# Feed forwards: the second half of the scaled row goes to a PSUM bank, and GpSimd splits two weight sums behind the last crossed part

## The reference

```
def swiglu(h, w_in, w_out):
    g, u = jnp.split(h @ w_in, 2, axis=-1)
    return (jax.nn.silu(g) * u) @ w_out
...
        h = h + g2 * swiglu(modulate(h, norm2_g[l], sh2, sc2), ffn_w_in[l], ffn_w_out[l])
        if need_ctx:
            hc = hc + cg2 * swiglu(modulate(hc, norm2_g[l], csh2, csc2), ffn_w_in[l], ffn_w_out[l])
```

## Time and profile before

| | |
|---|---|
| median of 3 runs | 4000.85 us (4000.85 to 4006.97) |
| the profiled execution's own time | 4003.02 us |
| its span | 4000.9 us |
| TensorE busy | 3700.5 us (92%) |
| VectorE busy | 2337.9 us (58%) |
| GpSimd busy | 1802.7 us (45%) |
| ScalarE busy | 1505.0 us (38%) |

### The profile page before, as it was taken

How to read it: one execution, slowest core, us unless ns; L and a number is a source line. 1 busy time by engine, 2 the same in 40 slices (tenths; PEclk the granted TensorE clock), 3 DMA queues, 4 the chain that set the end, 5 groups by cost and what they waited for, 6 DMA issues and landing times. The chain is left out here.

```text
span 4000.9 us, 82113 instructions
## 1 busy us (share of the span) xinstructions
PE 3700.5 (92%) x33646; PEld 3242.0 (81%) x33646; DVE 2337.9 (58%) x4324; ACT 1505.0 (38%) x2826; POOL 1802.7 (45%) x1226
## 2 busy tenths in 40 slices
PE   6998899999899899989799999979999999988997
PEld 5877799999677788868698888769999878668996
DVE  3345566666553766685557775276666640637665
ACT  3235333333365443332234443243333241644443
POOL 2201455554344777632233432155555332737884
PEclk8999999999999999989879999889999989989998
DMA  4223233332201444432201100223333211012331
GB/s 177 69 98 106 90 101 112 119 108 95 70 5 48 152 154 154 137 112 109 76 20 31 29 21 25 80 85 106 106 116 114 72 63 64 23 54 74 101 101 63
DMA packets 159555, 343.99 MB, mean 86 GB/s; under 512 B 33487, under 2 KB 89295, under 8 KB 158799
## 3 DMA queue, kind: packets, MB, share of 16 engines
q1 hardware_dynamic: 139311, 266.37, 20.2%
q10 hardware_dynamic: 19872, 72.36, 5.3%
HBM read 323.88 MB, written 16.93 MB: 85 GB/s over the span
## 5 line engine op out<-in xcount | busy, mean ns | idle before, releaser
L1450 POOL TENSOR_TENSOR feed_low<-feed_sums,feed_high 128x512 fp32r<-128x512 f32 x320 | 502.0, 1587 | 476.0 <-ACT feed_high L1444 468.0
L1450 POOL TENSOR_TENSOR feed_low<-ring,feed_high 128x512 fp32r<-128x512 f32 x448 | 596.2, 1347 | 193.6 <-ACT feed_high L1444 96.7
L1444 ACT ACTIVATE feed_high<-ring 128x512 fp32r<-128x512 f32 x448 | 278.5, 626 | 433.2 <-PE ps L1692 243.2
L1676 PE MATMUL ps<-hn_high,feed_high 128*128 128x384 f32 (+1 forms) x1280 | 401.9, 314 | 0.8 <-ACT feed_gate L1764 0.8
L1677 PE MATMUL ps<-hn_low,feed_high 128*128 128x384 f32 (+1 forms) x1280 | 395.4, 309 | 0.0
L1678 PE MATMUL ps<-hn_high,feed_low 128*128 128x384 f32 (+1 forms) x1280 | 395.3, 309 | 0.0
L1690 PE MATMUL ps<-feed_hid,feed_high 128*128 128x384 f32 (+1 forms) x1056 | 378.8, 359 | 13.6 <-DVE h L1874 6.1
L1691 PE MATMUL ps<-feed_hid,feed_high 128*128 128x384 f32 (+1 forms) x1056 | 375.9, 356 | 0.0
L1692 PE MATMUL ps<-feed_hid,feed_low 128*128 128x384 f32 (+1 forms) x1056 | 375.5, 356 | 0.0
L1444 ACT ACTIVATE feed_high<-feed_sums 128x512 fp32r<-128x512 f32 x320 | 189.3, 626 | 488.5 <-DVE feed_sums L1469 275.0
L1676 PE MATMUL ps<-cross_high,feed_high 128*128 128x384 f32 (+1 forms) x960 | 300.3, 313 | 22.7 <-issue 21.7
(11 more groups left out here) (639 smaller groups left out, 9489.1 us busy)
## 6 DMA issues: line engine op xcount, KB each, us to landing
feed_side_ring<-in_ada ACTq DMA_DIRECT2D x138, 512.0 KB, 4.3
ring<-in_ffn_g SPq DMA_DIRECT2D x88, 512.0 KB, 4.9
ring<-in_ffn_u SPq DMA_DIRECT2D x88, 512.0 KB, 3.7
ring<-in_ffn_d SPq DMA_DIRECT2D x88, 512.0 KB, 3.8
diff_side_ring<-in_ada SPq DMA_DIRECT2D x32, 512.0 KB, 4.2
ring<-in_od_in SPq DMA_DIRECT2D x24, 512.0 KB, 4.0
ring<-in_ev_in SPq DMA_DIRECT2D x23, 512.0 KB, 5.2
ring<-in_even_in SPq DMA_DIRECT2D x20, 512.0 KB, 4.1
```

The lines of the kernel that those rows point to most:

```text
L1444: act.activation(self.high[:, e % self.SLOTS, :], self.source(name, n), ACT.Copy).then_inc(self.high_ready, 1)
L1450: pool.tensor_tensor(self.low[:, slot, :], self.source(name, n), self.high[:, slot, :].bitcast(F32), ALU.subtract).then_inc(self.low_ready, 1)
L1676: pe.matmul(dst, high, vh, start=c == 0, stop=False)
```

## The change

It has three edits, all in the feed forward:
- `cross` scales the first half of the row into the SBUF scratch as before, and the second half into PSUM bank 6. All that reads the second half reads it there. The scaling is cut at half the tokens, so it has one instruction more in each part.
- The scratch handed to it is only half as wide.
- GpSimd's loop leaves out operand 11 after part 3. Operands 11 and 12 are split after the low part of part 4.

```
--- before.py
+++ after.py
     def cross(self, dve, c):
 
-        h, upper, lower = self.half, self.scratch, self.sq[:, c, :]
+        h, first, second, lower = self.half, self.scratch, self.k.ps[:, 6, 0:self.half], self.sq[:, c, :]
...
-        for a, b, s in spans(self.tokens):
-            dve.scalar_tensor_tensor(out=upper[:, a:b], in0=self.k.h[:, c, a:b], scalar=self.gains[:, c, s:s + 1],
-                                     in1=self.root[:, a:b], op0=ALU.mult, op1=ALU.mult)
+        for a, b, s in [(0, h, 0)] + self.second_half():
+            dve.scalar_tensor_tensor(out=second[:, a - h:b - h] if a else first, in0=self.k.h[:, c, a:b],
+                                     scalar=self.gains[:, c, s:s + 1], in1=self.root[:, a:b], op0=ALU.mult, op1=ALU.mult)
         dve.drain()
         for a, b, s in self.second_half():
             if s:
-                dve.scalar_tensor_tensor(out=t1[:, a - h:b - h], in0=upper[:, a:b], scalar=self.context_shifts[:, c:c + 1],
-                                         in1=upper[:, a - h:b - h], op0=ALU.add, op1=ALU.subtract)
+                dve.scalar_tensor_tensor(out=t1[:, a - h:b - h], in0=second[:, a - h:b - h], scalar=self.context_shifts[:, c:c + 1],
+                                         in1=first[:, a - h:b - h], op0=ALU.add, op1=ALU.subtract)
             else:
-                dve.tensor_tensor(t1[:, a - h:b - h], upper[:, a:b], upper[:, a - h:b - h], ALU.subtract)
+                dve.tensor_tensor(t1[:, a - h:b - h], second[:, a - h:b - h], first[:, a - h:b - h], ALU.subtract)
         for a, b, s in self.second_half():
             step, op = (self.shifts[:, c, s:s + 1], ALU.subtract) if shifted else (self.step_shifts[:, c, s:s + 1], ALU.add)
-            dve.scalar_tensor_tensor(out=t3[:, a - h:b - h], in0=lower[:, a:b], scalar=step, in1=upper[:, a:b], op0=op, op1=ALU.subtract)
+            dve.scalar_tensor_tensor(out=t3[:, a - h:b - h], in0=lower[:, a:b], scalar=step, in1=second[:, a - h:b - h], op0=op, op1=ALU.subtract)
...
-            norm = stream(st, vectors=vectors, fourth=fourth, scratch=upper[:, :])
+            norm = stream(st, vectors=vectors, fourth=fourth, scratch=upper[:, 0:H])
...
                 norm.low_cross(pool, c)
                 if c == 0:
                     operands.write_low(pool, 8)
-                operands.write_low(pool, 9 + c)
+                if c < 2:
+                    operands.write_low(pool, 9 + c)
+            operands.write_low(pool, 11)
+            operands.write_low(pool, 12)
             norm.low_fourth(pool)
```

## The result

The changed kernel takes 3971.1 us (median of 4 runs, 3967.0 to 3975.6), the kernel before 4001.9 beside it (4 runs, 4000.9 to 4007.0). The ratio is 0.9914, 95% interval 0.9887 to 0.9942: 0.86% faster, where 0.55% was predicted. A second series of the changed kernel gave 3970.6 and 0.9924 (0.9911 to 0.9937). The direction was right, and most of the gain is in the place that I had named; it is 34 us by the first ratio and 30 by the second (the medians differ by 30.8 and 29.0), where I had 22.2.

A forecast was written before the change was run, and what follows sets the result against it. TensorE, busy mostly, stops 21.7 us in the feed forwards for VectorE's crossed parts, held by GpSimd's SBUF lock. Chain 17.5 plus clock 4.9 minus swap 0.2 gives 22.2 us: 4000.85 to 3978.6, range 3968 to 3990 (own range 3973 to 3985).

The forecast's parts named there:

- 19.2 us free: VectorE's L1350, L1347 and L1353 over four crossed stretches: their cost without waiting behind GpSimd, against 58.5 us measured before.
- Rival E: VectorE's scaled second half: writing it to PSUM is slow and makes the kernel slower, 4010 us at 1.3 us; chance 0.04.
- the chain gains, 17.5 us: VectorE's crossed parts ahead of TensorE's first crossed product: they end 5.3, 3.0, 5.9 and 3.3 us earlier in four stages.
- the 39.3 us of waiting: Time L1350, L1347 and L1353 stand still behind GpSimd in four crossed stretches; all of it was to go from them.
- My walk: First stage's four crossed parts, turn by turn, with `t2` and the fourth sum still waiting for GpSimd: ends 5.3 us earlier.
- The clock: TensorE's granted clock stays up behind the first and third stages' shortened stops, giving 4.9 us; the fourth stays slow.
- The GpSimd swap: Moving operand 11's split behind low part 4 delays later splits by 1.3 us; cost 0.2 us, bounds 0 and 5.2.
- The sum: Whole kernel: 17.5 + 4.9 - 0.2 = 22.2 us gained, from the median 4000.85 to 3978.6 us.
- C: Crossed stretches: hardly any waiting comes back, stops shrink to TensorE's own pace, 33.6 us gained, 3967 us; chance 0.12.
- B: Crossed parts: waits move on more than walked or the PSUM write is dear; chain gains 9, about 3988 us; chance 0.22.
- D: TensorE's stops are set by low part 4 and the plain product, not crossed parts: no change, 4000 us; chance 0.07.
- The PSUM source: `t1` and `t3` reading PSUM: taken as costing nothing extra; the skill's 65 ns each would add 3.1 us, giving 3981.7.

The follow-up runs named there:

- cut_in_sbuf: Changed kernel with the scaled row's second half kept in SBUF instead of PSUM, same cut and GpSimd order: 3988.2 us, ratio 0.9981 to the kernel before.
- swap_only: Kernel before with only GpSimd's new order (operands 11 and 12 split after low part 4), row uncut in SBUF: 4010.5 us, ratio 1.0014.
- one_locked_swap_long: Changed kernel with, at 512 tokens, one instruction per part with two SBUF inputs and GpSimd's old order: 3970.5 us, ratio 0.9923 to the kernel before.
- after_third: Changed kernel, unedited, traced once more to see whether its stages repeat: the execution took 3976.0 us.
- psum_only: Changed kernel with GpSimd's order as in the kernel before (operand 11 split between low parts 3 and 4): 3974.2 us, ratio 0.9950 to the kernel before.
- swap_long_only: Changed kernel with GpSimd's new order only at 768 tokens, the old order at 512: 3970.3 us, ratio 0.9932 to the kernel before.
- psum_long_only: Changed kernel with the second half in PSUM only at 768 tokens, in SBUF at 512: 3975.1 us, ratio 0.9936 to the kernel before.
- one_locked: Changed kernel rewritten at 512 tokens so one instruction behind the scaling, not two, has both inputs in SBUF: 3969.9 us, ratio 0.9919 to the kernel before.

## Why the prediction was right and wrong

**The mechanism: right.** Which instructions stop standing still and by how much (19.2 us free), and that `ps<-h` costs no more than a write to SBUF (0.48 us for 256 columns): as written. The added scaling instruction makes a part 0.13 us longer, where I had 0.18. Rival E is out. `cut_in_sbuf` shows that the PSUM input itself does it, 17 us of the feeds.

**The step that failed: the chain gains, 17.5 us.** From before to after the time from the start of the crossed stretch to the first crossed product shrank by 6.3, 2.9, 6.9 and 5.0 us, 21.1 in all, where I had 5.3, 3.0, 5.9 and 3.3. That is 54% of the 39.3 us of waiting, where I had written less than half. VectorE's four parts alone shrank by 6.4, 4.2, 6.9 and 5.0, 22.5 in all: in the second stage the parts gained 4.2, but TensorE no longer waited for them and moved by 2.9, so that it meets my 3.0 is luck. My walk had the turns of the first stage right and their sizes a little too dear. It has 6.1, 6.65, 5.25 and 5.2 us for the four parts; they took 5.92, 6.08, 5.09 and 5.09. Part 2 makes half of that: `t2` asked 0.15 us earlier than walked, and `t2` and the fourth sum then took 1.78 and 1.48 us, their own 0.74 and 0.62 included, less than I had for two whole splits. Summed up, I let 21.8 of the 39.3 us be lost again, 2.9 of them to the added instructions, and 18.2 were: 13.7 as waits of `t2` and the fourth sum, 2.1 for the added instructions, 1.3 in the second stage, the rest in gaps. So the term that was too large is the waiting that comes back: some 19 us walked, 13.7 measured.

**The clock: right in size, then given back elsewhere.** Behind the first and third stop it stays 1.00, 2.4 us each by the matmuls of these two traces, as predicted. For the third stage that was the price of one execution: in the other two traces of the kernel before the clock there was 1.00 and 0.68 already. And a stop of 2.04 us that comes 21 us later in this stage has 0.68 behind it in the kernel after and had 1.00 in the first trace of before, which takes 1.1 us back. The means of three traces leave some 1 us for the third stage's clock, not 2.5. What I did not foresee is the attention. In both kernels TensorE stands still there four times within 15 us, for 0.8, 4.6, 1.8 and 0.8 us, and during the second of these stops the granted clock falls to 0.50. Windows of the kernel before and of the kernel after, over the whole slow stretch:

```profile
1122.70:1132.90 10.20, 5.89 (x28) 4.45 (x28) 4.91 (x17) 3.28 (x8) 1.83 (x1) 0.50 0.03 8
```

```profile
1111.50:1128.60 17.10, 11.28 (x55) 8.21 (x57) 8.46 (x28) 6.93 (x16) 4.49 (x3) 0.50 0.05 18
```

It lasts 10.2 us in the one and 17.1 in the other, where it goes on behind the last of the four stops. The attention takes 2.7 to 3.0 us more in all three traces of the changed kernel. Neither PSUM nor an earlier arrival settles it: `swap_only` and `cut_in_sbuf`, without PSUM, have 13.7 us of half clock there and 310.8 and 310.2 us of attention, and `one_locked_swap_long`, which comes there 9 us earlier than the kernel before, has 10.2 and 308.2, while `after_third`, 4 us earlier, has 17.1. Why the clock comes back sooner in one than in the other no run here tells.

**The GpSimd swap: mis-sized, -0.2 us for what is 2 in the fourth stage.** I named the thin cover at 512 tokens and its bound of 1.3 us, and then took 0.2. Behind low part 4 GpSimd does two splits before the low part of the fourth sums, so its whole row comes later: L1387 begins 1.6 us behind the first crossed product (3609.24 and 3607.61), with the old order 0.4 (3607.37 and 3606.97). No stop stands ahead of the product with the fourth sums. But some 12 us behind the first crossed product VectorE makes a sum of weights, L1467, with two inputs in SBUF. VectorE and GpSimd there, in the kernel after:

```profile
3619.43 1.17 DVE L1467 TENSOR_TENSOR feed_sums<-ring 128x512 f32<-128x512 f32 x1
```

```profile
3617.51 2.54 POOL L1450 TENSOR_TENSOR feed_low<-ring,feed_high 128x512 fp32r<-128x512 f32 x2 [0.19 <-issue]
```

and in `psum_only`:

```profile
3618.78 0.68 DVE L1467 TENSOR_TENSOR feed_sums<-ring 128x512 f32<-128x512 f32 x1
```

```profile
3615.64 2.55 POOL L1450 TENSOR_TENSOR feed_low<-ring,feed_high 128x512 fp32r<-128x512 f32 x2 [0.19 <-issue]
```

In the kernel after L1467 asks before the second split ends at 3620.05 and takes 0.49 us more; in `psum_only` the splits are over at 3618.19. All that VectorE does next is as much later, and the second stop, which ends with VectorE's `h`, is 0.47 us longer. The stretch from the first crossed product to the end is 3.0 us longer than in `psum_only` (335.9 and 332.8): 0.5 is this stop, and 2.5 the half clock behind it. The swap wins 0.8 us ahead and loses 3.0 behind, in the fourth stage alone; `psum_only` and `swap_long_only`, both with the old order there, have the short stop (1.62 us) and the clock at 1.00. The clock's part is not the swap's by itself: `cut_in_sbuf`, `psum_long_only` and `one_locked` have the swap and a second stop of 2.5 to 2.8 us with the clock 1.00 behind it, and lose 0.3 to 1.0 us there against the 332.8 of `psum_only`.

**The sum, against traces and against times.** In the three traces of each kernel the four feed forwards differ by 23.8 us (1820.9 and 1797.1), and the mean spans by 23.3 (3997.0 and 3973.7). The predicted 22.2 is within 2 us of that, and this closeness is luck: the chain gave 3.6 us more and the vanished stops of 0.58 us 2.2 that I did not have, while the third stage's clock gave 1.5 less, and the fourth stage and the attention took 3.0 and 2.9 back. The timed executions differ by more: all 11 of after have the mean 3971.3, and the three profiled ones, 3975.6, 3976.0 and 3976.1, are its three highest, while the profiled ones of before (3994.8, 3999.2 and 4003.0) lie in the midst of theirs. So some 6 us of the 29 to 31 lie in executions without a trace. The middle is where they could be: it varies from 937 to 948 us in kernels with the same code there, and more of it runs at 1.2 GHz where it is longer (granted clock 0.89 at 948.1, 0.91 at 936.9 and 937.0). The lora stage's stall is a rival that no run excludes: the nine traces in which L878 is not held have middles of 937 to 946 us, the five in which it is 942 to 962. Whether the changed kernel meets the better of these more often, or whether it is chance, stays open.

**The rivals.** C forecast 3967, nearer to the measured 3971.1 than my 3978.6, by a mechanism that did not happen: 13.7 us of waiting came back and the fourth stage kept its slow clock. B is out, the chain gave 21 and not 9. D is out by the timelines.

**The PSUM source.** The Trainium skill ("VectorE: DVE Perf Modes", The TRN2 errata) would make the 48 instructions with a PSUM source 3.1 us dearer (the estimate of the prediction). The rows don't show it: L1350 with 128 columns takes 0.29 us, 256 columns of it 0.42, the 256 of L1347 and L1353 0.47 to 0.48, and these are the lengths that I had derived from rows with SBUF inputs alone. L1350 took 0.29 and L1347 0.47 in the kernel before too, with both inputs in SBUF, where nothing held them.

## What to carry to other kernels

Where VectorE and GpSimd both work out of SBUF, an operand in a free PSUM bank freed an instruction from GpSimd's turns here at no cost that the rows show (the cut that it needed added 0.13 us a part). Do it for every instruction of the chain that can be so written: the ones left with two SBUF inputs inherited a third of the waiting (13.7 of 39.3 us), and `one_locked` shows that the algebra can be turned to leave a single one. A swap on GpSimd that wins 0.8 us ahead of a product is to be priced by which VectorE instructions with two SBUF inputs the later splits will then meet, in the shortest stage first, with the clock behind the stop that this lengthens.

Where single executions differ by 10 us, compare stages in the traces, not only spans; here most feed forwards repeat within 1 us.

## What the runs showed of the hardware beside that

**A VectorE instruction can lose several turns in a row.** In the lora stage of the kernel before L878 (one SBUF tensor input, no PSUM) asks at the same place while GpSimd has L799 and the two fills queued without a gap. The timelines of VectorE and GpSimd in the kernel before:

```profile
1725.52 5.31 DVE L878 TENSOR_SCALAR lora_norm_sq<-h,lora_norm_gains 128x256 f32<-128x256 f32 x1
```

```profile
1725.51 1.85 POOL L799 TENSOR_TENSOR hn_low<-lora_norm_sq,hn_high 128x768 fp32r<-128x768 f32 x1 [2.30 <-ACT hn_high L851]
1727.29 1.42 POOL L2901 MEMSET lora_pooled<- 128x1584 f32 x1
1728.66 2.03 POOL L2902 MEMSET mo<- 128x2313 f32 x1
```

It takes 5.31 us here and in `swap_only`, 3.33 in the second trace and 1.98 in the third, that is until the third, the second or the first GpSimd instruction is done; its free length is 0.35. In the kernel after it asks 0.34 us before L799 and takes 0.35. The Trainium skill ("SBUF — State Buffer", Who interferes with whom) has the lock and that the second comer blocks. By that rule L878, asking just behind L799, stands until L799 ends; that a waiting instruction can be passed over once and twice is what these rows add.

**Between full and half clock.** The granted clock over the 5.3 us behind a stop of TensorE, all stops from the first crossed product to the end of a feed forward, all traces together:

| stop, us | granted clock behind it |
|---|---|
| 1.5 to 1.8 | 1.00, always |
| 2.0 to 3.0 | 30 stops: 1.00 in 11, 0.68 to 0.71 in 16, 0.52 to 0.60 in 3 |
| 3.2 to 4.0 | 0.68 to 0.73 in 4, 1.00 in one (behind 3.41) |
| 4.9 to 5.0 | 0.50 or 0.51 in 7, 0.73 in one |
| 5.7 to 9.0 | 0.50 to 0.61 |

A longer stop goes with a lower clock, but the length of one stop alone does not tell it: 2.03 us was followed by 0.68 in one trace and by 1.00 in another, and 3.41 by 1.00.
